# Down product of a decoder layer: seven quarter products for eight (Strassen's scheme) on 15 of 16 pairs of K tiles, with the activations' low parts on GpSimd

## The reference

```python
x = x + merged @ w_out
f = rmsnorm(x, norm2_w) @ w_up                 # (1088 x 1024) @ (1024 x 4096)
x = x + jnp.square(jax.nn.relu(f)) @ w_down    # (1088 x 4096) @ (4096 x 1024)
...
y_prompt = rmsnorm(xp, norm_f_w)
y_sample = rmsnorm(xs, norm_f_w)
```

## Time and profile before

| | us |
|---|---|
| median of 3 runs | 1656.51 (1656.39 to 1656.58) |
| span of the profiled execution | 1654.3 |
| TensorE busy | 1644.5 (99%) |
| VectorE busy | 691.6 (42%) |
| GpSimd busy | 568.9 (34%) |
| ScalarE busy | 516.3 (31%) |

### The profile page before, as it was taken

One profiled execution on the slowest core, in us unless ns is written; L12 is line 12 of the kernel. 1 busy time (PEld: TensorE's weight loads), 2 busy tenths in 40 slices (PEclk: granted clock), 3 DMA queues, 4 the chain that ended last, 5 costly groups with the idle time before them and its releaser, 6 DMA issues.

```text
span 1654.3 us, 24985 instructions
## 1 busy us (share of the span) xinstructions
PE 1644.5 (99%) x9956; PEld 1520.8 (92%) x9956; DVE 691.6 (42%) x1156; ACT 516.3 (31%) x1001; POOL 568.9 (34%) x402
## 2 busy tenths in 40 slices
PE   9999999999999999999999999999999999999998
PEld 8999999999988889999889998899888998899987
DVE  7785877859521222466334330032211331022333
ACT  6565655656322222422245220022100220012111
POOL 5212212112212211232884334733347324652510
PEclk9999999999999999999999999999999999999999
DMA  5202112021276677442552111321113111221211
GB/s 161 66 26 66 40 39 71 22 61 44 94 244 194 206 231 230 163 145 91 172 178 77 52 52 64 102 65 51 52 64 115 47 43 64 89 83 46 90 51 57
DMA packets 145007, 157.55 MB, mean 95 GB/s; under 512 B 9120, under 2 KB 99900, under 8 KB 144893
## 3 DMA queue, kind: packets, MB, share of 16 engines
q1 hardware_dynamic: 144746, 155.93, 29.6%
q10 hardware_dynamic: 146, 0.04, 0.0%
HBM read 136.96 MB, written 18.98 MB: 94 GB/s over the span
## 4 chain that ended last, share of the span: by engine, by line
PE 89%; DVE 6%; ACT 3%; issue 1%; POOL 0%; DVEq 0%; ACTq 0%; POOLq 0%
PE ps L1126 51%; PE ps L1418 10%; PE ps L1423 10%; PE ps L1421 9%; DVE sp L1909 2%; PE ps L1320 2%; DVE zc L1901 1%; PE ps L1276 1%; PE ps L1286 1%; PE ps L1364 1%; PE ps L1332 1%; ACT sp L1612 1%; PE ps L1303 1%; PE ps L1302 1%; DVE br L1857 1%
## 5 line engine op out<-in xcount | busy, mean ns | idle before, releaser
L1126 PE MATMUL ps<-xh,wh 128*128 128x364 f32 (+1 forms) x956 | 323.7, 339 | 0.7 <-DVE xl L1882 0.6
L1126 PE MATMUL ps<-xh,wl 128*128 128x364 f32 (+1 forms) x956 | 313.9, 328 | 0.0
L1126 PE MATMUL ps<-xl,wh 128*128 128x364 f32 (+1 forms) x956 | 313.8, 328 | 0.0
L1113 POOL TENSOR_TENSOR wl<-raw,wh 128x1024 fp32r<-128x1024 f32 x106 | 256.8, 2422 | 19.1 <-POOL wh L1110 19.1
L1126 PE MATMUL ps<-yh,wh 128*128 128x384 f32 (+1 forms) x768 | 250.8, 327 | 0.6 <-POOL wl L1113 0.6
L1126 PE MATMUL ps<-yh,wl 128*128 128x384 f32 (+1 forms) x768 | 250.5, 326 | 0.0
L1126 PE MATMUL ps<-yl,wh 128*128 128x384 f32 (+1 forms) x768 | 250.3, 326 | 0.0
L1110 POOL CAST wh<-raw 128x1024 fp32r<-128x1024 f32 x106 | 110.6, 1043 | 404.3 <-issue 383.0
L1736 ACT ACTIVATE ts<-tt 128x384 f32<-128x384 f32 (+1 forms) x96 | 48.8, 508 | 553.8 <-DVE tt L2090 553.6
L1027 POOL CAST wh<-raw 128x1024 fp32r<-128x1024 f32 x48 | 50.8, 1057 | 479.5 <-issue 205.3
L1126 PEld LDWEIGHTS ps<-xh,wh 128*128 128x128 f32 x956 | 179.8, 188 | 17.0 <-issue 15.3
(11 more groups left out here) (190 smaller groups left out, 2629.6 us busy)
## 6 DMA issues: line engine op xcount, KB each, us to landing
raw<-in_w_down SPq DMA_DIRECT2D x112, 256.0 KB, 2.9
raw<-in_w_in SPq DMA_DIRECT2D x80, 256.0 KB, 3.5
cache<-in_cache_k SPq DMA_DIRECT2D x64, 256.0 KB, 3.7
cache<-in_cache_v SPq DMA_DIRECT2D x64, 256.0 KB, 3.6
raw<-in_w_up SPq DMA_DIRECT2D x64, 256.0 KB, 3.2
raw<-in_w_out SPq DMA_DIRECT2D x48, 256.0 KB, 2.9
gates<-gst SPq DMA_DIRECT2D x16, 544.0 KB, 6.1
gb<-gates SPq DMA_DIRECT2D x16, 544.0 KB, 5.6
```

The lines of the kernel that those rows point to most:

```text
L1113: g.tensor_tensor(low[:, :], raw[n % 3][:, :], f32(high[:, :]), ALU.subtract).then_inc(w_split, 1)
L1126: ins = mm(out, lhs[:, k * P:(k + 1) * P], rhs[:, x], start=(first and a == 0 and m == 0), stop=(last and a == n - 1 and m == 2))
```

## The change

The last tiles of K are no longer taken in quarters but in 16 pairs ("twins") of K tiles. For twins 0 to 14 the operands are cut in two ways: the two K tiles, the two halves of the 1024 prompt tokens, and the two halves of the 1024 output columns. That is a 2 x 2 product of blocks, and Strassen's scheme (in Winograd's form) makes it with seven quarter products (512 tokens x 128 x 512 columns) where eight stand in the plain one. Its operands are sums and differences: VectorE makes four of the activations (`sums_`), GpSimd four of the weights (`tw`); the pair of `w_down` tiles comes into `raw_d`, which is single. ScalarE rounds the seven activation operands into `a_hi`, and GpSimd makes their low parts `a_lo` (before, VectorE made `hl`). GpSimd also splits the eight weight operands in halves of 512 columns, in a ring of five places (N_RING = 5), five operands ahead of the first up tile (N_SOON = 5) and three behind it. Each quarter product goes from PSUM to `x1` by two adds on VectorE, of two banks each. The sample tokens ("few") are not in the scheme: 8 matmuls a twin. Twin 15 is done in the plain way at the very end, block after block ("block"), with each block's final norm behind it. Twin n's products stand behind the up tiles of twin n + 1.

```diff
+        N_TWIN = D_FF // (2 * P)
+        LAST_TWIN = N_TWIN - 1
+        PREP = (0, "few0", "few1", 1, 6, 3, 4, 2, 5)
+        LOWS = tuple(x for x in PREP if x not in ("few0", "few1"))
+        BESIDE_UP = (2, 2, 2, 2, 1, 0)
+        TARGET = ((0, 0), (0, 0), (0, 1), (1, 1), (1, 1), (0, 1), (1, 0))
...
+        for n in range(1, N_TWIN):
+            tail += [("sum", n - 1, k) for k in range(4)]
+            todo = list(PREP)
+            for m in range(6):
+                e = 2 * n + m // 3, m % 3
+                tail += [("up", *e), ("relu", *e)]
+                for _ in range(BESIDE_UP[m]):
+                    tail.append(("prep", n - 1, todo.pop(0)))
+            if n == LAST_TWIN:
+                tail.append(("end_prep",))
+            tail += [("prod", n - 1, 0), ("few", n - 1, 0)]
+            tail += [("prod", n - 1, p) for p in range(1, N_WAY)]
+            tail.append(("few", n - 1, 1))
+        tail += [("end_few",), ("wf_spread",)]
...
+        OP_LAST = [("few", 0)] + [("prod", p, 1) for p in range(1, 5)] + [("few", 1), ("prod", 6, 1), ("few", 1)]
+        N_OP = len(OP_LAST)
...
+            def load_twin(n):
+                if n:
+                    sp_.wait_ge(d_lo, N_OP * n)
...
+                for s in range(2):
+                    sp_.dma_start(raw_d[s][:, :], wdn[:, 2 * n + s, :]).then_inc(d_in, 16)
...
+            def down_op(n, k):
+                if of >= N_RING:
+                    pool.wait_ge(step_done, op_used(of - N_RING))
+                if k == 2:
+                    g.tensor_tensor(tw[0][:, :], b12, b11, ALU.subtract).then_inc(t_made, 1)
+                    pool.wait_ge(t_made, 4 * n + 1)
+                    g.tensor_tensor(tw[1][:, :], b22, tw[0][:, :], ALU.subtract).then_inc(t_made, 1)
+                    pool.wait_ge(t_made, 4 * n + 2)
...
+                g.tensor_copy(high, src).then_inc(d_hi, 1)
+                pool.wait_ge(d_hi, of + 1)
+                g.tensor_tensor(low, src, f32(high), ALU.subtract).then_inc(d_lo, 1)
+                pool.wait_ge(d_lo, of + 1)
...
+            def low_of(n, x):
+                pool.wait_ge(op_hi, prep_no[n, x] + 1)
+                g.tensor_tensor(a_lo[x][:, :], op_source(n, x), f32(a_hi[x][:, :]), ALU.subtract).then_inc(op_lo, 1)
+            for n in CYCLES:
+                for k in range(N_SOON):
+                    down_op(n, k)
+                    for x in LOWS[max(0, 2 * k - 3):max(0, 2 * k - 1)]:
+                        low_of(n, x)
+                if 2 * n + 4 < 2 * N_TWIN:
+                    tail_tile(N_OUT + 2 * n + 4)
+                for k in range(N_SOON, N_OP):
+                    down_op(n, k)
+                if 2 * n + 5 < 2 * N_TWIN:
+                    tail_tile(N_OUT + 2 * n + 5)
+            pool.wait_ge(d_in, 32 * LAST_TWIN + 32)
+            pool.wait_ge(step_done, LAST_UP)
+            for s in range(2):
+                g.tensor_copy(end_wh[s][:, :], raw_d[s][:, :]).then_inc(end_w_hi, 1)
+                pool.wait_ge(end_w_hi, s + 1)
+                g.tensor_tensor(end_wl[s][:, :], raw_d[s][:, :], f32(end_wh[s][:, :]), ALU.subtract).then_inc(end_w_lo, 1)
+            for s in range(2):
+                pool.wait_ge(end_hi, s + 1)
+                g.tensor_tensor(end_l[s][:, :], hf[LAST_TWIN % 2][s][:, 0:SEQ], f32(end_h[s][:, 0:SEQ]), ALU.subtract).then_inc(end_lo, 1)
...
+                elif e[0] == "prod":
+                    pe.wait_ge(op_lo, len(LOWS) * n + LOWS.index(p) + 1)
+                    pe.wait_ge(d_lo, of + 1)
+                    for q in range(2):
+                        pe.wait_ge(step_free, prod_bank_read(n, p, q))
+                        for b in (2 * q, 2 * q + 1):
+                            mm(out, a_hi[p][:, x], w, start=not onto, stop=False, skip_group_check=onto)
+                            mm(out, a_lo[p][:, x], w, start=False, stop=False, skip_group_check=onto)
+                            ins = mm(out, a_hi[p][:, x], lo_w, start=False, stop=True, skip_group_check=onto)
+                        ins.then_inc(step_done, 1)
...
+                elif e[0] == "block":
+                    for s in range(2):
+                        if t < 2:
+                            pe.wait_ge(end_w_lo, s + 1)
+                            pe.wait_ge(end_lo, s + 1)
```

More of the change, by code:

```diff
@@ L185, in hybrid_layer @@
-        assert 2 * N_BIG + 3 <= 8 * WIDE // (4 * D)
+        HS = SEQ // 2
+        ROW = 4 * HS
+        N_WAY = 7
+        at = r1
+        a_hi = [place(f"a_hi{p}", [P, HS], F32R, at + 2 * p * ROW) for p in range(N_WAY)]
+        a_lo = [place(f"a_lo{p}", [P, HS], F32R, at + (2 * p + 1) * ROW) for p in range(N_WAY)]
+        at += 2 * N_WAY * ROW
+        few = [place(f"few{s}", [P, 2 * SMP], F32R, at + s * 8 * SMP) for s in range(2)]
+        at += 16 * SMP
+        hf = [[place(f"hf{t}_{s}", [P, NTOK], F32, at + (2 * t + s) * 4 * NTOK) for s in range(2)] for t in range(2)]
@@ new lines, in hybrid_layer @@
+        at += 16 * NTOK
+        tw = [place(f"tw{n}", [P, HS], F32, at + n * ROW) for n in range(2)]
+        at += 2 * ROW
+        spare = [at]
+        assert at + ROW <= r1l + 4 * 4 * SEQ
+        at += ROW
+        raw_d = [place(f"raw_d{s}", [P, D], F32, at + s * 4 * D) for s in range(2)]
+        at += 8 * D
+        sums_ = [place(f"sum{n}", [P, HS], F32, at + n * ROW) for n in range(4)]
+        assert at + 4 * ROW <= r1 + 8 * WIDE
+        spare += [rest, rest + ROW]
+        N_RING = 5
@@ new lines, in hybrid_layer @@
+        while len(spare) < 2 * N_RING:
+            spare.append((END + 31) // 32 * 32)
+            END = spare[-1] + ROW
+        assert END <= nc.sbuf_usable_end
+        d_hi_at = [place(f"d_hi{n}", [P, HS], F32R, spare[2 * n]) for n in range(N_RING)]
+        d_lo_at = [place(f"d_lo{n}", [P, HS], F32R, spare[2 * n + 1]) for n in range(N_RING)]
+        at = ry
+        end_h = [place(f"end_h{s}", [P, HW], F32R, at + s * 4 * HW) for s in range(2)]
+        at += 8 * HW
+        end_l = [place(f"end_l{s}", [P, SEQ], F32R, at + s * 4 * SEQ) for s in range(2)]
@@ L1420, in by_rows @@
                     if b < NB:
-                        mm(out, low[:, k * SEQ + b * P:k * SEQ + b * P + P], w, start=False, stop=False)
+                        mm(out, ml[:, k * SEQ + b * P:k * SEQ + b * P + P], w, start=False, stop=False)
                 if "low" in parts:
@@ L1462, in _ @@
                 elif e[0] == "block":
                     _, b, h = e
[L1464 to L1468 removed]
+                    t = BLOCKS.index(e)
+                    out = bank(BLOCK_BANK[t % 6])
```

454 lines of the change are left out of this document (282 added, 172 removed).

## The result

The changed kernel takes 1636.01 us (median of 4, 1634.91 to 1636.24), the kernel before 1656.45 (4 runs, 1656.25 to 1656.58): a ratio of 0.9876 [0.9862, 0.989], a gain of 20.4 us. The forecast was 1627.0, a gain of 29.5. The time lies outside the range that the prediction called its own (1623 to 1632) and inside the wider one (1621 to 1641), and 9 us of the gain are missing.

The account below looks back on a forecast made before the run. The feed-forward part was taken as bound by TensorE's matmul count: -40.8 (matmuls) + 6.7 (twin 15) + 5.1 (norms) - 0.4 to -0.9 (quarter waits) = -29.5, so 1627.0 us from 1656.51; own range 1623 to 1632, wider 1621 to 1641.

Parts of the forecast that it names:

- The count: Down products on TensorE: 92 matmuls a pair of K tiles for 104, 180 fewer in all, worth 40.8 us.
- I keep 0.2267: Product matmuls on TensorE: 0.2267 us each as before, so 20.86 us a twin and a cycle of 44.64 us.
- waits that I didn't see: TensorE in the cycles: unseen waits of 0.2 to 0.6 us a cycle, 1630 to 1636; within the first rival's chance 0.15.
- VectorE: Adds out of PSUM: 1.22 us a pair add, 18.5 us a twin against TensorE's 20.86, so it keeps up.
- The first rival: VectorE's pair adds slower than 1.22 us, or unseen TensorE waits: together 1630 to 1642, chance 0.15.
- GpSimd: Casts, subtractions and up tiles: 40.3 us a cycle against 44.64, 4.3 us to spare, so TensorE never waits for it.
- One item I had called hidden: Reload of raw_d in the cycle: two DMAs of 256 KB land in 3 to 4 us, during the second up tile.
- the rival of the other sign: GpSimd becomes the bound and the kernel is slower, from 6.3 us more a cycle: 1660 to 1700 or above, chance 0.04.
- Lows on GpSimd or VectorE: Activation low parts: on VectorE they add 4.8 us to its cycle and take 9 from GpSimd's; the sum doesn't move.
- VectorE against GpSimd: SBUF-only VectorE instructions don't run beside GpSimd's: 0 on the path, up to 1.3 us for a sum inside the room.
- The wait for twin 15: After twin 14, TensorE stands until twin 15 is loaded and split: 6.7 us net of 3 matmuls.
- The end: Last twin's stretch: 6.7 us wait, 101 more matmuls in 22.9 us, and an end 5.1 us later behind the last matmul.

Follow-up runs that it names:

- Run 5: The changed kernel with the seven displaced operand-ring buffers put at 192 modulo 512 bytes, the activations' place in the row: 1629.0 us, 0.9836.
- run 8: The changed kernel with one weight subtraction of each twin made five times more on GpSimd: 1687.44 us (one run).
- run 7: The changed kernel with the seven low parts of each twin moved from GpSimd back to VectorE: 1635.24 us, 0.9871.
- run 3: The changed kernel with 22 useless matmuls in the hole where TensorE waits for twin 15: 1633.08 us, 0.9859.
- Run 6: The changed kernel with the seven ring buffers at 320 modulo 512 bytes, the other three keeping 192: 1633.85 us (one run).
- run 9: The changed kernel with the ring at 320 modulo 512 and all SBUF buffers moved up by 128 bytes: 1628.89 us (one run).
- run 2: The kernel before with its four weight tiles wh and wl moved by 32 bytes: 1669.69 us, 1.0085.
- Run 1: The changed kernel with its operand ring started at a multiple of 64 bytes instead of 32: 1632.53 us, 0.9856.
- run 10: The changed kernel with one weight subtraction of each twin made two times more on GpSimd: 1636.2 us (one run).

## Why the prediction was right or wrong

**The count: right.** 180 matmuls fewer, and nothing else on TensorE.

**"All operands of a product are 128 x 128 against 512 columns as before, so I keep 0.2267": this is the step that failed.** The mechanism and the count held, the pace was 0.2322. It is worth 0.50 us a twin, 7.5 us in 15, of which up tiles that are 0.08 us a cycle quicker than forecast give 1.1 back. Run 5, which changes only addresses, gives 0.2273 and takes 6.5 us out of the cycles. The 0.0006 that are left, 0.06 us a twin, are my reading and not a cost of the change: a whole down stage of the kernel before, from 984.8 to 1079.53, is 0.2276 us a matmul with 0.2 us of waiting in it, and I took six matmuls for all. The shape was the same, the place wasn't, and the diff shows the place (the ring is allocated at the end of the used space, not where `wh` was). In the prediction 1630 to 1636 was reserved for waits that I didn't see. The time landed at the edge of that band, but no wait caused it: that the wide range held was luck.

**VectorE: right.** A pair add was put at 1.22 us; the changed kernel's source line has (count, ns min/median/max):

```profile
L2245 DVE TENSOR_TENSOR x<-ps,x x210: 1224/1225/1227, 939.6 to 1589.5; 128x1024 f32<-128x1024 f32 x105
```

The first rival (1.38 and more) has no support: two banks in one instruction cost what one piece of 1024 costs, and no wait of TensorE for VectorE appears in the cycles.

**GpSimd: right, in both senses.** The line through 8 and 1024 columns gave 1.29 and 0.61 us; by shape the changed kernel has (busy us, mean ns, idle before):

```profile
L1250 POOL TENSOR_TENSOR d_lo<-raw_d,d_hi 128x512 fp32r<-128x512 f32 x60 | 80.3, 1339 | 4.8
L1250 POOL TENSOR_TENSOR d_lo<-tw,d_hi 128x512 fp32r<-128x512 f32 x60 | 77.6, 1293 | 4.8
L1259 POOL TENSOR_TENSOR a_lo<-sum,a_hi 128x512 fp32r<-128x512 f32 x60 | 76.5, 1296 | 6.1 <-POOL d_lo L1250 5.7 <-ACT a_hi L1940 0.4
...
L1248 POOL CAST d_hi<-tw 128x512 fp32r<-128x512 f32 x60 | 36.8, 613 | 2.9
```

Its idle time ahead of low 0 is 56.4 / 14 = 4.0 us a cycle (4.4 forecast). One item I had called hidden shows: `raw_d`'s reload makes GpSimd wait 25.0 / 14 = 1.8 us a cycle. I had misread its size. The earlier trace rows are for the kernel before, which loads a tile in two halves of 256 KB; here a DMA brings a whole tile of 512 KB. The DMA view of the changed kernel has (KB, median us from issue to landing):

```profile
raw_d<-in_w_down SPq DMA_DIRECT2D x32, 512.0 KB, 4.5
```

The view of the kernel before has a line of that size, which would have given the right figure:

```profile
x<-in_x_prompt SPq DMA_DIRECT2D x8, 512.0 KB, 4.7
```

The wait comes out of the room and not out of the time. That the room was real is run 8: with 6.85 us more GpSimd is the bound and the kernel is slower than before, the rival of the other sign. By the settled cycles it decides from 4.4 (room) + 20.4 / 15 (gain left, 1.4) = 5.8 us more a cycle, where 6.3 was the forecast; run 8's first cycle, its end and its low clock say that the true point lies lower.

**Lows on GpSimd or VectorE: right.** The Trainium skill's rule in "GPSIMD Engine Reference", section "Elementwise — side-by-side cycle accounting", would keep them on VectorE. The rows agree with its ground fully only where VectorE is alone (0.68 us against GpSimd's 1.296). In run 7 VectorE's busy time rises by 130 us for 105 of them, 1.24 us each: they last 0.98 us in the mean, and the rest is other instructions that grew. Neither is on the path, and the time is the same.

**VectorE against GpSimd: right.** The exclusion of the earlier trace rows is in the changed kernel too, and it costs nothing. The four sums have these means (by shape), where the earlier trace rows have 0.692:

```profile
L2313 DVE TENSOR_TENSOR sum<-hf 128x512 f32<-128x512 f32 x15 | 16.9, 1129 | 0.0
L2313 DVE TENSOR_TENSOR sum<-hf,hf 128x512 f32<-128x512 f32 x15 | 16.1, 1073 | 0.6 <-ACT hf L1926 0.6
L2313 DVE TENSOR_TENSOR sum<-sum,hf 128x512 f32<-128x512 f32 x15 | 14.3, 954 | 0.0
L2313 DVE TENSOR_TENSOR sum<-hf,sum 128x512 f32<-128x512 f32 x15 | 12.3, 822 | 0.5
```

That is up to 0.44 us each where 1.3 was allowed.

**The wait for twin 15: 7.4 us for 7.4, the mechanism right and the equal number in part luck.** Counted from the start of cycle 14 (1545.18), operand 7 was split at 36.1 as forecast, but the load, with its 512 KB tiles, landed at 41.0 and not at 39.7. The splits behind it then took 11.5 us for the 12.3 allowed, and TensorE itself was 0.5 late, so that the two ends of the hole moved alike. Missing was what the hole does to TensorE's clock. I had the hole's length and didn't ask what the engine does after it. It is a term of 2.6 us in "The end" (run 3).

**The norms at the end: right within 0.7 us.** 10.6 from the last matmul's end for 11.3.

**The three waits between quarters: gone,** too small to see apart.

Left open: what the moving operand must lie level with, and why. Run 6 says that it is the moving buffer's own place that decides for its matmuls, run 9 that this place is relative to something that moved along. The stationary operands are the first candidate; that run 2's up stages kept their pace with shifted stationary tiles doesn't fit it simply, though the operands of those stages were not level to begin with. Run 1 says that 64 bytes off cost half of what 32 and 128 do. Not tried: the stationary operands moved alone, and other distances, 256 bytes among them.

## What to carry to other kernels

A matmul saved is worth its pace, and the pace depends on where a new buffer lies: after adding one, compare starts of like matmuls before and after, and if they differ with no wait between them, move the buffer. Here the same place in a 512 byte row as the other operands brought the pace back; the true period was not found. Before a DMA's time is taken from a row, compare its size with the row's. A single buffer that is harmless in a loop becomes a hole where the loop ends, and the hole costs its length and the slow clock behind it. When blocks at the end become short, price the serial work behind them on each engine, also on the one it is moved to.

## What the runs showed of the hardware that was not expected

- A float32r matmul of 512 columns starts 0.2273 us after the last one with the ring level with the other operands, some 0.2297 with it 64 bytes off (slots 2 to 4), 0.233 with it 32 or 128 bytes off (runs 5, 1, the changed kernel, 6). Within one product it is the matmul that streams the misplaced buffer that is late, 234 ns beside 227 (run 6). The same offset in the kernel before costs 13.3 us of 1656 (run 2).
- The granted clock fell to 0.50 when TensorE had stood for 3.0 us. It stayed there over three matmuls, another wait of 0.7 us and 13 more matmuls 0.43 us apart, 10.2 us in all; 22 useless matmuls in the gap kept it at 1.00 (run 3). Behind the same hole it lasted 6.8 us in runs 5 and 10.
- VectorE's adds with a PSUM operand keep their 1.224 to 1.227 us in all 210 cases beside a GpSimd that is busy for more than half of the time.
